# Adaptive rows beside the gates, and loads begun one stage ahead, in a hybrid diffusion block

## The reference, cut to what matters

```
mod = silu(c) @ w_ada + b_ada                  # 6 rows: sh1 sc1 g1 sh2 sc2 g2
h   = layer_norm(x) * (1 + sc1) + sh1          # the same for the context, by c_ctx
z, xbc, dt, q, k, v, g = split(h @ w_in)
y_ssd  = rms_norm(ssd(silu(conv(xbc)), dt) * silu(z), ssd_norm_w)
y_attn = windowed_attention(rope(q), rope(k), v, sink)
m  = sigmoid(g)[ssd] * (y_ssd @ w_ssd_br) + sigmoid(g)[attn] * (y_attn @ w_attn_br)
x1 = layer_norm(alpha * x + g1 * (m @ w_o + b_o)) * ln1_g + ln1_b
h2 = layer_norm(x1) * (1 + sc2) + sh2
out = layer_norm(alpha * x1 + g2 * experts(h2)) * ln2_g + ln2_b
```

## Time and profile before

| | before |
|---|---|
| median of 3 runs | 2930.75 us (2930.63 to 2934.76) |
| profiled execution | 2933.16 us, span 2931.5 us |
| TensorE matmul busy | 2504.5 us, 85% |
| VectorE busy | 1597.0 us, 54% |
| ACT busy | 1061.7 us, 36% |
| POOL busy | 705.8 us, 24% |
| granted TensorE clock, mean | 0.915 |

### The profile page before, as it was taken

How to read it: one execution, slowest core, us unless ns; L and a number is a source line. 1 busy time by engine, 2 the same in 40 slices (tenths; PEclk the granted TensorE clock), 3 DMA queues, 4 the chain that set the end, 5 groups by cost and what they waited for, 6 DMA issues and landing times. The chain is left out here.

```text
span 2931.5 us, 31293 instructions
## 1 busy us (share of the span) xinstructions
PE 2504.5 (85%) x11848; PEld 1972.9 (67%) x11848; DVE 1597.0 (54%) x1674; ACT 1061.7 (36%) x1349; POOL 705.8 (24%) x487
## 2 busy tenths in 40 slices
PE   6799999999898996975989659698885499999992
PEld 2588888778697885653656448576474388888881
DVE  4455554431143665763556352532254699999994
ACT  3333333121131113541334341310232377777772
POOL 0001000010002434994992000000042212222113
PEclk8799999999999998996999869899697699999996
DMA  4333333342225867949564255543333599999994
GB/s 188 97 109 116 117 117 108 115 144 86 89 88 197 299 241 247 308 164 202 148 157 88 54 167 150 161 118 94 119 115 113 222 375 397 391 395 398 398 362 143
DMA packets 307553, 556.80 MB, mean 190 GB/s; under 512 B 22121, under 2 KB 212025, under 8 KB 283953
## 3 DMA queue, kind: packets, MB, share of 16 engines
q1 hardware_dynamic: 277938, 431.61, 43.3%
q0 software_dynamic: 27200, 115.10, 12.1%
q10 hardware_dynamic: 2304, 8.62, 0.8%
HBM read 434.22 MB, written 120.79 MB: 189 GB/s over the span
## 5 line engine op out<-in xcount | busy, mean ns | idle before, releaser
L2412 DVE TENSOR_TENSOR e_wlo<-e_w,e_whi 128x2048 fp32r<-128x2048 f32 x188 | 425.7, 2290 | 43.5 <-ACT e_whi L2365 42.2
L2365 ACT CAST e_whi<-e_w 128x2048 fp32r<-128x2048 f32 x192 | 366.3, 1915 | 120.8 <-PE e_gu L2525 83.5
L386 PE MATMUL f_lat<-h_hi,w_hi 128*128 128x512 f32 x800 | 254.4, 399 | 0.3 <-DVE w_lo L522 0.3
L386 PE MATMUL f_lat<-h_lo,w_hi 128*128 128x512 f32 x800 | 250.7, 394 | 0.0
L386 PE MATMUL f_lat<-h_hi,w_lo 128*128 128x512 f32 x800 | 250.6, 394 | 0.0
L522 DVE TENSOR_TENSOR w_lo<-w_raw,w_hi 128x1024 fp32r<-128x1024 f32 x50 | 61.3, 1225 | 216.9 <-ACT w_hi L447 216.9
L1889 PE MATMUL b_acc<-b_hi,b_whi 128*128 128x512 f32 x384 | 151.4, 394 | 14.0 <-DVE b_lo L1840 14.0
L1579 DVE CUSTOM_DVE_ANT_0 a_masked<-a_a_ps,a_mask 128x640 f32<-128x640 f32 x128 | 105.5, 825 | 99.3 <-PE a_a_ps L1483 95.9
L1510 PE MATMUL a_c_ps<-a_prob,a_v 128*128 128x512 f32 x304 | 157.8, 602 | 0.0
L386 PEld LDWEIGHTS f_lat<-h_hi,w_hi 128*128 128x128 f32 x800 | 136.0, 188 | 30.5 <-issue 4.8
L386 PEld LDWEIGHTS f_lat<-h_hi,w_lo 128*128 128x128 f32 x800 | 136.0, 188 | 27.7
(11 more groups left out here) (346 smaller groups left out, 5627.8 us busy)
## 6 DMA issues: line engine op xcount, KB each, us to landing
e_w<-in_w_gate_up SPq DMA_DIRECT2D x128, 1024.0 KB, 10.4
e_w<-in_w_down SPq DMA_DIRECT2D x64, 1024.0 KB, 8.7
w_raw<-in_w_in SPq DMA_DIRECT2D x50, 512.0 KB, 4.0
t_space<-xbcT POOLq DMA_DIRECT2D x18, 1280.0 KB, 6.4
before<-t_space SPq DMA_DIRECT2D x16, 1024.0 KB, 4.2
y_before<-before SPq DMA_DIRECT2D x64, 256.0 KB, 6.1
a_ada_w<-in_w_ada POOLq DMA_DIRECT2D x32, 512.0 KB, 4.1
b_w<-in_w_ssd_br SPq DMA_DIRECT2D x16, 1024.0 KB, 5.6
```

What stands on the lines that cost most here:

```text
L386: mm = nc.tensor.matmul(o, weights[:, b, k, :], part[:, k, a:a + n], start=(k == 0 and n_pass == 0), stop=(k == KT - 1 and n_pass == 2))
L2365: nc.scalar.copy(whi[:, slot % SPLIT], w[:, slot]).then_inc(w_hi, 1)
L2412: V.tensor_tensor(wlo[:, slot % SPLIT], w[:, slot], whi[:, slot % SPLIT].bitcast(F32), ALU.subtract).then_inc(w_split, 1)
```

## The change

It has five parts.

1. front_stage loads the modulation weights first, from both queues, and tokens behind them. ACT modulates seven pieces of a tile, VectorE the eighth. Behind the tokens, SP also loads the first two weight tiles of the projection (class First). The row buffer shrinks to two.
2. project_f_stage waits for each table only where it is used. Its gate stores move from POOL's queue to SP's. In their place POOL makes the ada rows: the 32 parts of 0.5 MB in three of the q/k buffers, added onto conv_acc, with the bias loaded into its first row. TensorE sums over the partitions after gates 5, 9, 13 and 15, VectorE copies the row, SP stores it in memory (mod). The stage ends when all four are stored.
3. attention_stage has no ada work. With chunk 3, SP loads the branch stage's constants, first two y tiles and first weights (class Later) between the queries and the inverse rows.
4. branch_stage finds those loaded. In its second half, SP loads the four tiles of w_o ahead of the second feature tile's weights (the y buffers' space is theirs).
5. residual_stage finds w_o loaded; the seven spread rows are replaced by six broadcast DMAs (0.5 MB each) from mod and the inputs, issued in ACT's queue; expert_stage reads g2 from mod. The calls of recycle(), which frees semaphores, stand at other seams.

```diff
+                load_w(sp, 0)
+                load_w(sp, 2)
+                for n in range(1, NCHUNK, 2):
+                    load_x(sp, n)
+                first.load(s, sp)
...
+    ON_ACT = KT - 1
...
-                load_x(0)
-                act.dma_start(ident[:], s.squares[:, 0:P]).then_inc(ident_in, 16)
+                load_w(act, 1)
                 act.wait_ge(cond_in, 32)
                 nc.scalar.activation(act_c[:], cond[:], ACT.Silu).then_inc(silu_done, 1)
-                for n in range(1, NCHUNK):
-                    load_x(n)
+                load_w(act, 3)
+                for n in range(0, NCHUNK, 2):
...
+                    V.tensor_scalar(h[:, n % 2, KT - 1, :], tp[:, n % TR, KT - 1, :], colm[:, 1, which, KT - 1:KT], colm[:, 0, which, KT - 1:KT],
+                                    ALU.mult, ALU.add).then_inc(h_rest, 1)
+                    dve.wait_ge(h_rest, n + 1)
...
+        ada_w = (qhi[:, 0, 0:D].bitcast(F32), qhi[:, 1, 0:D].bitcast(F32), qlo[:, 0, 0:D].bitcast(F32))
+        ada_sum, ada_row = (conv[:, 0, 0:D], conv[:, 1, 0:D]), turned[0:1, 0, 0:D]
...
+        SUM_AFTER = {5: 0, 9: 1, 13: 2}
...
+                for n in range(NG):
+                    sp.wait_ge(w_free, NX + NQK + n + 1)
+                    sp.dma_start(w[:, n % 2], wv[:, :, G0 + P * n:G0 + P * n + P]).then_inc(w_in[n % 2], 16)
+                    if n >= 3:
+                        store_gate(n - 3)
+                    if n - 2 in SUM_AFTER:
+                        store_rest(SUM_AFTER[n - 2])
                 ahead.load(s, sp)
...
+                def sum_rest(c):
+                    pe.wait_ge(ada_step, KT * c + KT)
+                    if c == 0:
+                        pe.wait_ge(ones_made, 1)
+                        pe.wait_ge(rot_step, 2 * NQK)
+                    else:
+                        pe.wait_ge(ada_made, c)
+                    for half in range(2):
+                        mm = nc.tensor.matmul(tp[0:1, 512 * half:512 * half + 512], ones[:], ada_sum[c % 2][:, 512 * half:512 * half + 512], start=True, stop=True)
+                    mm.then_inc(ada_summed, 1)
+
+                for n in range(2, NG):
+                    product(NX + NQK + n, n % 2, False)
+                    if n in SUM_AFTER:
+                        sum_rest(SUM_AFTER[n])
+                sum_rest(REST - 1)
...
+                def load_part(j):
+                    c, k = divmod(j, KT)
+                    if j >= 3:
+                        pool.wait_ge(ada_step, j - 2)
+                    pool.dma_start(ada_w[j % 3], wa[:, k, (2 + c) * D:(3 + c) * D]).then_inc(ada_in[j % 3], 16)
+
+                def clear_sum(c):
+                    if c >= 2:
+                        pool.wait_ge(ada_summed, c - 1)
+                    nc.gpsimd.memset(ada_sum[c % 2], 0.0).then_inc(ada_blank, 1)
+                    pool.wait_ge(ada_blank, c + 1)
+                    pool.dma_start(ada_sum[c % 2][0:1], s.x["b_ada"][:, (2 + c) * D:(3 + c) * D]).then_inc(ada_bias_in, 16)
+
+                def add_part(j):
+                    c, k = divmod(j, KT)
+                    pool.wait_ge(ada_in[j % 3], 16 * (j // 3) + 16)
+                    nc.gpsimd.tensor_scalar(ada_w[j % 3], ada_w[j % 3], cond[:, k:k + 1], None, ALU.mult).then_inc(ada_scaled, 1)
+                    pool.wait_ge(ada_scaled, j + 1)
+                    if k == 0:
+                        pool.wait_ge(ada_bias_in, 16 * c + 16)
+                    pool.wait_ge(ada_step, j)
+                    nc.gpsimd.tensor_tensor(ada_sum[c % 2], ada_sum[c % 2], ada_w[j % 3], ALU.add).then_inc(ada_step, 1)
+
                 for b in range(2):
...
+                clear_sum(0)
+                for j in range(2):
+                    load_part(j)
+                for j in range(PARTS):
+                    if j + 2 < PARTS:
+                        load_part(j + 2)
+                    if j % KT == 4 and j // KT + 1 < REST:
+                        clear_sum(j // KT + 1)
+                    add_part(j)
+                pool.wait_ge(ada_out, 16 * REST)
...
+        self.wo = own(st, nc, "l_wo", [P, KT, D])
+        flat = self.wo[:].rearrange("p k n -> p (k n)")
...
+        self.y = flat[:, 0:2 * D_INNER].rearrange("p (b n) -> p b n", b=2)
...
+    def load_branch(self, s, sp, yT):
+        KY = D_INNER // P
+        sp.dma_start(self.ident[:], s.squares[:, 0:P]).then_inc(self.const_in, 16)
+        sp.dma_start(self.normw[:], s.x["normw"]).then_inc(self.const_in, 16)
+        for n in range(2):
+            sp.dma_start(self.y[:, n], yT[n * P:n * P + P, :]).then_inc(self.y_in[n], 16)
+        sp.dma_start(self.w[:, 0:KY], s.x["w_ssd_br"][0].rearrange("(k p) n -> p k n", p=P)[:, :, 0:P]).then_inc(self.w_in, 16)
+        sp.dma_start(self.w[:, KY:], s.x["w_attn_br"][0].rearrange("(k p) n -> p k n", p=P)[:, :, 0:P]).then_inc(self.w_in, 16)
...
+                        if n == 3:
+                            later.load_branch(s, sp, yT)
                         spread_inverse(n - 1)
...
+                    if half:
+                        sp.wait_ge(y_lo, LCHUNK)
+                        sp.wait_ge(a_split, LCHUNK + 2)
+                        for j in range(4):
+                            later.load_wo(s, sp, j)
...
-                load_w(0)
                 load_m(0)
-                load_w(1)
-                for n in range(2, 4):
-                    sp.wait_ge(w_split, n - 1)
-                    load_w(n)
                 load_m(1)
                 load_x(0)
                 load_x(1)
+                sp.dma_start(ident[:], s.squares[:, 0:P]).then_inc(const_in, 16)
...
-                for j in range(len(ROWS)):
-                    spread_row(j)
                 pe.wait_ge(w_split, 4)
...
                 for n in range(4):
-                    act.wait_ge(w_in[n % 2], 16 * (n // 2) + 16)
-                    nc.scalar.copy(whi[:, :, WP * n:WP * n + WP], w[:, n % 2]).then_inc(w_hi, 1)
-                    if n >= 1:
-                        keep_row(2 * n - 2)
-                        keep_row(2 * n - 1)
+                    act.wait_ge(later.wo_in[n], 16)
+                    nc.scalar.copy(whi[:, :, WP * n:WP * n + WP], w[:, :, WP * n:WP * n + WP]).then_inc(w_hi, 1)
+                    if n == 0:
+                        for j, row in ((G1, mod[0:1, 2 * D:3 * D]), (B_O, s.x["b_o"]), (LN_G, s.x["ln1_g"]), (LN_B, s.x["ln1_b"]),
+                                       (SC2, mod[0:1, 4 * D:5 * D]), (SH2, mod[0:1, 3 * D:4 * D])):
+                            act.dma_start(rowv[:, j], row.to_broadcast([P, D])).then_inc(rows_in, 16)
                     if n < 2:
                         split_hi(n)
-                    if n == 3:
-                        keep_row(6)
-                        act.wait_ge(rows_kept, 7)
```

More of the change, by code:

```diff
@@ L139, in bank, with __init__, load, front_stage @@
     return stack.enter_context(nc.psum_tensor(name, shape, dtype))
-def front_stage(s, hi, lo, cond_cols):
+class First:
+    def __init__(self, s, st):
+        self.w = own(st, s.nc, "w_raw", [P, 2, KT, P])
+        self.w_in = [s.sem(f"f_w_in{b}") for b in range(2)]
+    def load(self, s, sp):
+        wv = s.x["w_in"][0].rearrange("(k p) n -> p k n", p=P)
+        for b in range(2):
+            sp.dma_start(self.w[:, b], wv[:, :, XBC0 + P * b:XBC0 + P * b + P]).then_inc(self.w_in[b], 16)
+def front_stage(s, hi, lo, first, cond_cols):
     nc = s.nc
@@ L154, in front_stage @@
         bias, ones = own(st, nc, "n_bias", [1, 2 * D]), own(st, nc, "n_ones", [1, 2])
-        row = own(st, nc, "n_row", [2, BLOCKS, 512])
+        row = own(st, nc, "n_row", [2, 2, 512])
         colm = own(st, nc, "n_cols", [P, 2, 2, KT])
@@ L312, in project_f_stage @@
         taps = own(st, nc, "conv_taps", [P, NX, CONV_W + 1])
-        w = own(st, nc, "w_raw", [P, 2, KT, P])
+        w, w_in = first.w, first.w_in
         whi = own(st, nc, "w_hi", [P, 2, KT, P], F32R)
@@ L336, in project_f_stage @@
         ctx_turned = s.sem("f_ctx_turned")
+        cond_in, ones_made, ada_in = s.sem("f_cond_in"), s.sem("f_ones_made"), [s.sem(f"f_ada_in{b}") for b in range(3)]
+        gate_out = [s.sem(f"f_gate_out{b}") for b in range(2)]
+        ada_blank, ada_bias_in = s.sem("f_ada_blank"), s.sem("f_ada_bias_in")
+        ada_scaled, ada_step, ada_summed, ada_made, ada_out = (s.sem(f"f_ada_{n}") for n in ("scaled", "step", "summed", "made", "out"))
         rot_step = s.sem("f_rot_step")
@@ L360, in _ @@
                 sp.dma_start(squares[:], s.squares.rearrange("p (a q) -> p a q", q=P)[:, 0:5, :]).then_inc(tables_in, 16)
[L361 to L365, removed]
+                sp.dma_start(taps[:], s.x["taps"]).then_inc(taps_in, 16)
+                sp.dma_start(cos[:], s.cosine).then_inc(turns_in, 16)
+                sp.dma_start(sin[:], s.sine).then_inc(turns_in, 16)
+                sp.dma_start(cond[:], cond_cols).then_inc(cond_in, 16)
+                for col, f0, n in ((XBC0, 0, NX), (Q0, NX, NQK)):
```

(12 more changed lines are left out.)

270 lines of the change are left out of this document (117 added, 153 removed).

## The result

The changed kernel takes 2959.67 us, the median of 4 runs (2958.61 to 2963.0), for 2932.76 of the kernel before, measured again beside it (4 runs, 2930.63 to 2937.08): a ratio of 1.0092, 95% interval 1.0074 to 1.0109. It is slower by 27 us, where 3 us less were forecast and 2945 was the upper end of the range; the slowest rival gave 2943. The profiled execution of it took 2959.06 us, span 2957.4, which is 25.9 more than that of before.

What follows compares the result with a forecast made beforehand. TensorE was taken as busy inside most stages, with open time at the seams. About 72 us of gains met 69 of losses, a sum of −3, forecasting 2928 us, own range 2918 to 2938, with rivals 2910 to 2945.

Steps and rivals of the forecast that it cites:

- the slowest rival: Gates: 14 splits of about 1.2 us on VectorE stop POOL, 17 us on its chain; 2943, chance 0.17.
- The head: Front stage and start of the projection: weights first and tables gating only their users give −6.5 and −8.
- the sum's −4.3 for the modulation's start: Head: first token tile at about 26, ten VectorE tiles take 25.5, so modulation starts near 52.6, 4.3 earlier.
- The gates: 32 ada parts of 6.23 us on POOL outlast 145 us of gates; next stage starts +57.5 later, ±4.
- The port: Gates: VectorE's two-input split and POOL share an SBUF port; taken as +1.5, the skill's rule being whole-instruction lockout.
- Attention: POOL's parts and ada loads gone, but early branch loads delay the inverse rows: sum −10.5, from −22 to −6.
- the start of the branch stage: First y tile already there, the 6.3 us wait goes and following tiles come about 2 earlier: −8, from −5 to −9.
- w_o ahead of the weights: Branch stage, half 2: 4.2 MB of w_o ahead of weights 9 delay their split: +10, from 0 to +12.
- The residual stage: Weights resident, no row spread: first product 16.5 us behind the start for 55.6, −39, from −35 to −42.
- the stalls in SP's queue don't bite: Attention and branch stage: transfers spread over rings, neither inverse nor w(9) late; −12 more, 2916; chance 0.15.
- the rows cost nothing beside the gates: Gates: the change does what it says, which would need parts of 4.4 us; 2869, chance 0.05.

Runs made afterwards that it cites:

- two experiments, 14 and 12 us: From the changed kernel: branch stage's loads issued behind the inverse rows, 2945.42 us; in another run, w_o issued behind the last branch weights, 2947.62 us.

## Why the prediction was wrong, point by point

- **The head**, −14.5 forecast, −10.7 measured. The step that failed is the sum's −4.3 for the modulation's start, which measured −0.6: it took VectorE's chain without a gap from the first tile, but VectorE waited 4.1 us for the second. With that chain done 2.9 us earlier the start moved less than 1 us, because TensorE's chain of four weight blocks ends at 52.7 in both runs; the forecast had not worked that chain out.
- **The gates**, +59 forecast, +71.0 measured. The mechanism and the four waits were right, their sizes within 3 us. The term was mis-sized in three places: from the last q/k store to the first multiply 12.6 us for 10.6; the chain 210.5 for 202.2; from the last add to the next stage 12.2 for 10.1. The store itself came 9.6 earlier, not with the full 10.7 of the head. Those are 2.0 + 8.3 + 2.1 + 1.1, less the 1.5 that the forecast had taken for the port: the 12.0 of the miss. The chain's 8.3 are the slower rival at half its size: POOL's stalls, where the rival had 17. That the splits did not all stop POOL is seen in the trace: of twelve splits of w beside the chain, three (each behind a copy) held an add up by 2.0 and one by 0.4, three waited 1.3 to 1.5 themselves for a running add, and the other five cost the chain less than 0.1.
- **The port.** The rule of the Trainium skill that was weighed there (SBUF — State Buffer, on who interferes with whom) is what the trace now shows where an add or a wide split is running: a split behind a running add ends at 669.06 for 667.99 + 1.1, a multiply behind a running wide split takes 4.47 for 2.85. For a split behind a running multiply it doesn't hold as it stands. By the rule the splits at 712.03 and 766.27 would have waited until the multiplies around them ended, at 712.96 and 766.88; both took a plain 1.22. Here the measurement decides.
- **Attention**, right in kind; with the start of the branch stage −15.4 for −16.8. The late inverse cost 13.1 (50.8 for 37.7), where 10 to 12 were worked out.
- **w_o ahead of the weights**, +10 less 2 forecast, +9.0 measured, 8.4 of it in one wait. Right.
- **The residual stage**, −39 forecast, −29.2 measured. The step that failed: the sum 4 x 2.3 + 1.9 + 3 + gaps = 16.5 has no wait for the tiles of m, and leaves the broadcasts out, as they "are wanted only behind the first product". They are, but they were issued beside the m tiles and delayed these (ACT waited 5.1 and 5.9 us), and ACT's order puts two casts of m ahead of the last casts of w_o: 23.2 us. Moved, the first product comes 15.8 us behind the start. The 3.3 us behind the first product are a term that the forecast did not have; the moved broadcasts did not take them away (143.9 us for 144.1).
- **The rest**, +1.5 at the end for 0: 1.0 of it lies between the residual and the expert stage, where a call of recycle() now stands. That this call is the cause was not tried.

The rivals: that the stalls in SP's queue don't bite fell by two experiments, 14 and 12 us. That POOL is stopped by the splits came half true. That the rows cost nothing beside the gates did not hold with the parts on POOL, and with them on VectorE it holds but for 9.9 us. The miss as a whole is that gains and losses near 70 us were set against each other as if each were known to 4; two of them were off by 10 and 12 the same way, and the measured time lies beyond the forecast and all its rivals.

## What to carry to other kernels

Before work is put beside a stage as cover, its chain on its own engine is to be set against the stage's length: here 32 x 6.28 us beside 145 us, while VectorE, idle for 10 of each 11 us, does the same part in 1.28. A load that is begun early goes into the queue behind, not ahead of, whatever the present stage waits for next, and a bulk load that is wanted late is issued behind the small one that is wanted first. When all that is right the parts of such a change add up, 90 us here. A forecast made of large gains against large losses is only as good as its worst term: two terms off by a fifth and a quarter moved this one by 22 us.

## What the runs showed of the hardware

An add on POOL and a two-input subtract (a split) on VectorE hold each other up. In all twelve places in the changed kernel and in the run with the copy on ACT where a split of w came upon a running add, it ended 1.07 to 1.09 us behind the add, for a plain length of 1.2. An add that waited for a split ended 2.26 or 2.27 us behind it in all five places of the changed kernel, three of them with the copy ahead of the split; its plain length is 2.4. With POOL's multiply it is not the same. Splits that began 0.2 to 0.7 us into one ended 2.2 us behind its start (1.56 to 2.05 us long), and those that began 1.9 us or more into one took their plain 1.22. The first two rows are of the run with the copy on ACT, the last two of the changed kernel:

```profile
723.14 2.86 POOL L711 TENSOR_SCALAR qk_hi<-qk_hi,f_cond 128x1024 f32<-128x1024 f32 x1
723.79 1.56 DVE L611 TENSOR_TENSOR w_lo<-w_raw,w_hi 128x1024 fp32r<-128x1024 f32 x1 [8.53 <-ACT w_hi L524]
```

```profile
710.11 2.85 POOL L711 TENSOR_SCALAR qk_hi<-qk_hi,f_cond 128x1024 f32<-128x1024 f32 x1
712.03 1.22 DVE L602 TENSOR_TENSOR w_lo<-w_raw,w_hi 128x1024 fp32r<-128x1024 f32 x1 [11.39 <-ACT w_hi L524]
```

TensorE's sum of four small products takes 3.57 us behind a wait of 5 to 25 us and 1.88 where TensorE has been at work without one. The stretch from the last gate to the next stage, which holds one such wait, has a granted clock of 0.51, near the lower level of 1.2 GHz; the 10 us around the first sum in the run with the parts on VectorE have 1.00. The view's columns are those of the earlier trace rows:

```profile
831.00:866.00 35.00, 3.57 (x4) 0.34 (x4) 1.21 (x1) 0.00 (x0) 22.30 (x11) 0.51 0.13 45
```
